# RWKV chunks of a hybrid decoder layer: sixteen at once with crosswise odd ones, and the state carried by transition matrices

## The reference

```python
    def step(s, inp):
        r_t, w_t, k_t, v_t, a_t, b_t = inp
        sa = jnp.einsum('nhvk,nhk->nhv', s, a_t)
        s = (s * w_t[:, :, None, :] + sa[..., None] * b_t[:, :, None, :]
             + v_t[..., None] * k_t[:, :, None, :])
        return s, jnp.einsum('nhvk,nhk->nhv', s, r_t)
```

## Time and profile before

| | us |
|---|---|
| median of 3 runs | 2684.76 |
| lowest, highest | 2681.96, 2686.89 |
| the profiled execution | 2676.91 |
| its span | 2675.2 |

### The profile page before, as it was taken

One profiled execution on the slowest core, in us unless ns is written; L12 is line 12 of the kernel. 1 busy time (PEld: TensorE's weight loads), 2 busy tenths in 40 slices (PEclk: granted clock), 3 DMA queues, 4 the chain that ended last, 5 costly groups with the idle time before them and its releaser, 6 DMA issues.

```text
span 2675.2 us, 39291 instructions
## 1 busy us (share of the span) xinstructions
PE 2428.9 (91%) x17425; PEld 1629.9 (61%) x17425; DVE 925.3 (35%) x1626; ACT 457.0 (17%) x946; POOL 158.9 (6%) x269
## 2 busy tenths in 40 slices
PE   5998999898888898888879997999999999999994
PEld 3665665557656766756756664666666666666563
DVE  3962441035325415415514333333331013333222
ACT  4114121122113113113130001111110001111002
POOL 2700000000000000000100000000000000000001
PEclk8999999999998998998979998999999999999997
DMA  6101233410020020011033311111101011110101
GB/s 220 60 20 41 78 120 111 132 56 16 11 58 15 8 61 15 8 38 46 3 137 106 128 32 32 32 33 33 33 29 44 24 64 33 33 33 25 36 20 65
DMA packets 111367, 139.72 MB, mean 52 GB/s; under 512 B 14818, under 2 KB 85975, under 8 KB 111184
## 3 DMA queue, kind: packets, MB, share of 16 engines
q1 hardware_dynamic: 96512, 115.38, 13.3%
q10 hardware_dynamic: 10992, 15.21, 1.6%
q0 software_dynamic: 3696, 6.64, 0.9%
HBM read 117.59 MB, written 19.61 MB: 51 GB/s over the span
## 4 chain that ended last, share of the span: by engine, by line
PE 79%; DVE 11%; ACT 4%; DMA 3%; issue 2%; DVEq 0%; ACTq 0%; SPq 0%; POOL 0%; POOLq 0%
PE ps L623 77%; DVE arena L1669 5%; DVE arena L1672 2%; DMA W<-in_w_in_dram 2%; PE ps L627 1%; DMA arena<-in_x_prompt_dram 1%; ACT Y L1437 1%; DVE arena L2100 1%; ACT arena L1316 0%; DMA Y<-in_x_prompt_dram 0%; DVE hT L1672 0%; DVE hT L1669 0%; DVE arena L2037 0%; ACT arena L1362 0%; DVE s5v L1669 0%
## 5 line engine op out<-in xcount | busy, mean ns | idle before, releaser
L623 PE MATMUL ps<-hT,W 128*128 128x352 f32 x4368 | 1337.1, 467 | 53.7 <-DMA W<-in_w_in_dram 17.8
L623 PEld LDWEIGHTS ps<-hT,W 128*128 128x128 f32 x4368 | 837.0, 193 | 528.8 <-issue 58.3
L623 PE MATMUL ps<-arena,W 128*128 128x352 f32 x1440 | 432.0, 463 | 14.7 <-DVE arena L1669 11.9
L623 PE MATMUL ps<-arena 64*64 64x64 f32 (+6 forms) x8744 | 354.6, 232 | 55.2 <-DVE arena L1669 22.0
L623 PEld LDWEIGHTS ps<-arena,W 128*128 128x128 f32 x1440 | 276.1, 192 | 170.1 <-DVE arena L1669 12.5
L623 PEld LDWEIGHTS ps<-arena 64*64 64x64 f32 (+3 forms) x8744 | 300.7, 137 | 115.7 <-issue 43.0
L1316 ACT ACTIVATE arena<-ps 128x512 f32<-128x512 f32 (+7 forms) x235 | 113.2, 489 | 523.1 <-PE ps L623 318.9
L2214 DVE TENSOR_SCALAR Y<-Y,PAR 128x1024 f32<-128x1024 f32 x88 | 49.0, 557 | 426.4 <-ACT Y L1316 424.7
L1316 ACT ACTIVATE Y<-ps 128x352 f32<-128x352 f32 (+3 forms) x220 | 69.9, 350 | 715.2 <-PE ps L623 536.5
L1669 DVE TENSOR_TENSOR arena<-arena 128x1056 f32<-128x1056 f32 (+6 forms) x181 | 166.8, 922 | 59.8 <-PE ps L623 44.9
L1669 DVE TENSOR_TENSOR arena<-ps,arena 128x256 f32<-128x256 f32 (+3 forms) x188 | 99.0, 527 | 220.4 <-PE ps L623 164.0
(11 more groups left out here) (250 smaller groups left out, 995.7 us busy)
## 6 DMA issues: line engine op xcount, KB each, us to landing
W<-in_w_ada_dram SPq DMA_DIRECT2D x12, 2048.0 KB, 9.4
W<-in_w_up_dram SPq DMA_DIRECT2D x22, 1024.0 KB, 6.5
gates<-arena ACTq DMA_DIRECT2D x72, 176.0 KB, 1.8
arena<-gates SPq DMA_DIRECT2D x24, 528.0 KB, 3.5
W<-in_w_in_dram SPq DMA_DIRECT2D x17, 512.0 KB, 4.9
W<-in_w_in_dram SPq DMA_DIRECT2D x4, 1536.0 KB, 7.1
W<-in_w_down_dram SPq DMA_DIRECT2D x4, 1536.0 KB, 6.6
W<-in_w_in_dram SPq DMA_DIRECT2D x5, 1024.0 KB, 6.5
```

The source lines that it names most:

```text
L623: return nc.tensor.matmul(out, lhsT, rhs, start=start, stop=stop, skip_group_check=True)
```

## The change

All 16 chunks of a pass are handled together, and odd chunks cross: where an operand lies on the partitions of head h, the product of an odd chunk is written to the other half (side), or the other way round, while two chunks next to each other write different banks. Exceptions are the transposed products of the levels (zt) and the turn of A, which stay in their own half, and the chain. A level works in two halves of eight chunks, with X and XT updated as 512 columns at a time. X is preset by ACT with the identity, and DVE writes the first factors over it with a predicated copy; XT is made by turning X on PE instead of from LA.

After level 5 four sets of products over all 16 chunks make, besides the old quantities, Gm (a transition matrix for each chunk, with the identity added) and R + YT.LA in ARp, and put the state-free part of outputs and of state updates into PSUM. The chain is then one accumulating product of Gm with the last state, and one DVE operation that scales it by PC into Sb, for 15 steps; the second product of a step adds the state's part to the output. Vt, Bt, Kt and the others get new places in the arena (VB, W0, U0, YT, Gm, Sb), partly over Bp, Kp, Vp and Z, and decode gets its own small tiles (dX, dXT, dLT, dYb, dLTm).

In decode gate group 5 goes to bank 7, group 6 is cut after three k steps instead of four and its first part moved ahead of the wait for dec_made 2, group 7 runs whole before the wait for dec_made 4, group 8 is cut in two, ahead of the output head sums and behind the turn of the decode states. The last prompt state is turned at the end of the pass. ACT has one more instruction a pass, the fill of X.

PE's core of the change:

```diff
-                for bt in range(2):
-                    for x, (b, src) in enumerate(((0, Vp), (1, Bp), (2, Kp))):
-                        take(b)
-                        for c in range(8):
-                            m = heads(lambda hp: mm(pb[b][hp, 64 * c:64 * c + 64], src[hp, 8 * bt + c, :], idS[hp, :]))
...
+                def both(bt):
+                    for c in range(8 * bt, 8 * bt + 8):
+                        for hh in range(2):
+                            yield c, c % 2, c % 8 // 2, half_of(hh), side(c, hh)
+
+                take(0, 1)
                 for bt in range(2):
+                    for c, par_, i, hp, sd in both(bt):
+                        m = mm(pb[par_][sd, col64(c // 2)], ARp[hp, c, 0, :], Bp[hp, c, :])
+                m.then_inc(sem("la_done"), 1)
+                give("la_ev", 0, 1)
+
+                def with_a_r(src, bt):
+                    b = 4 + 2 * bt
+                    take(b, b + 1)
+                    for c, par_, i, hp, sd in both(bt):
+                        m = mm(pb[b + par_][sd, P * i:P * (i + 1)], src[hp, c, :],
+                               ARp[hp, c, :, :].rearrange("p a b -> p (a b)"))
...
+                with_a_r(Bp, 0)
+                with_a_r(Bp, 1)
+                take(2, 3)
...
+                values_b(0)
+                with_a_r(Kp, 0)
+                with_a_r(Kp, 1)
+                values_b(1)
+                pe.wait_ge(sem("la_ev"), 5 * j + 1)
+                for bt in range(2):
+                    take(2 * bt, 2 * bt + 1)
+                    for c, par_, i, hp, sd in both(bt):
+                        m = mm(pb[2 * bt + par_][hp, col64(i)], X[sd, pos(c), :], idS[sd, :])
+                    m.then_inc(sem("tk_done"), 1)
+                    give("tk_ev", 2 * bt, 2 * bt + 1)
+                take(4, 5)
+                for bt in range(2):
+                    for c, par_, i, hp, sd in both(bt):
+                        m = mm(pb[4 + bt][hp, col64(4 * par_ + i)], ARp[hp, c, 0, :], idS[hp, :])
+                m.then_inc(sem("tk_done"), 1)
...
+                def yy(l, s):
+                    pe.wait_ge(sem("lt_ready"), level_at(j, l, s))
+                    if l > 1:
+                        pe.wait_ge(sem("zx_ev"), 8 * j + 2 * (l - 2) + s + 1)
+                    take(2 * s, 2 * s + 1)
+                    for c, par_, i, hp, sd in both(s):
+                        m = mm(pb[2 * s + par_][hp, col64(i)], LT[sd, lane(c), :], X[sd, pos(c), :])
...
+                def zt(l, s):
+                    zt_ready(l, s)
+                    take(4 + s)
+                    for c, par_, i, hp, sd in both(s):
+                        m = mm(pb[4 + s][hp, col64(4 * par_ + i)], Yb[hp, lane(c), :], XT[hp, lane(c), :])
...
+                yy(1, 0)
+                yy(1, 1)
+                for l in range(1, last):
+                    for s in range(2):
+                        zx(l, s)
+                        zt(l, s)
+                        yy(l + 1, s)
...
+                take(6, 7)
+                for s in range(2):
+                    for c, par_, i, hp, sd in both(s):
+                        m = mm(pb[6 + par_][hp, col64(c // 2)], YT[sd, pos(c), :], vb(c, 1)[sd, :])
+                m.then_inc(sem("gm_done"), 1)
+                give("gm_ev", 6, 7)
...
+                for c in range(1, 16):
+                    par_, i = c % 2, c // 2
+                    pe.wait_ge(sem("s_ready"), 16 * j + c)
+                    if c == 1:
+                        pe.wait_ge(sem("gm_ev"), 2 * j + 1)
+                    heads(lambda hp: mm(pb[4 + par_][hp, col64(i)], Gm[hp, pos(c), :], Sb[hp, c - 1, :], False, True))\
+                        .then_inc(sem("ds_done"), 1)
+                    if c == 1:
+                        pe.wait_ge(sem("y_part"), j + 1)
+                        pe.wait_ge(sem("gm_ev"), 2 * j + 2)
+                    m = heads(lambda hp: mm(pb[par_][hp, col64(i)], Sb[hp, c - 1, :], ARp[hp, c, 1, :], False, True))
+                m.then_inc(sem("ry_done"), 1)
```

DVE's and ACT's part of it, the mask on POOL and the decode order:

```diff
@@ POOL
-                        if n > 2:
-                            pool.wait_ge(sem("yy_done"), 2 * (n - 2))
-                        pool.tensor_tensor(LT[n % 2], LA[:, :, 0, :],
+                for l in range(1, LEVELS):
+                    for s in range(2):
+                        if l == 1:
+                            pool.wait_ge(sem("la_ev"), 5 * j + s + 2)
+                        else:
+                            pool.wait_ge(sem("yy_done"), level_at(j, l - 1, s))
+                        pool.tensor_tensor(LT[:, 8 * s:8 * s + 8, :], LA[:, 8 * s:8 * s + 8, 0, :],
@@ ACT
+                copy(X[:, :, :], idS[:, :].unsqueeze(1).to_broadcast([P, 16, RCH])).then_inc(sem("x_unit"), 1)
...
+                act.wait_ge(sem("tk_done"), 6 * (j + 1))
+                copy(LTm[:].rearrange("p c t -> p (c t)"), ps[:, 4:6, :].rearrange("p b t -> p (b t)"))\
+                    .then_inc(sem("tk_ev"), 1)
@@ DVE
+                step(v.copy_predicated(X[:, :, :], m_l0[:].bitcast(words).unsqueeze(1).to_broadcast([P, 16, RCH]),
+                                       ps[:, 0:2, :].rearrange("p b (c t) -> p (b c) t", t=RCH)), "la_ev")
...
+                def carry(c):
+                    step(v.tensor_scalar(Sb[:, c, :], pb[4 + c % 2][:, col64(c // 2)], PC[:, c:c + 1], None, MUL), "s_ready")
...
+                for c in range(1, 16):
+                    dve.wait_ge(sem("ds_done"), 15 * j + c)
+                    carry(c)
@@ PE, decode
-                gates_part(8 + j, 5, 0, KT, 2)
+                gates_part(8 + j, 5, 0, KT)
...
+                gates_part(8 + j, 6, 0, 3)
                 pe.wait_ge(sem("dec_made"), 4 * j + 2)
...
-                gates_part(8 + j, 6, 0, KT // 2)
+                gates_part(8 + j, 6, 3, KT)
...
-                gates_part(8 + j, 6, KT // 2, KT)
+                gates_part(8 + j, 7, 0, KT)
...
-                gates_part(8 + j, 7, 0, KT, 3)
+                gates_part(8 + j, 8, 0, 4)
...
-                gates_part(8 + j, 8, 0, KT, 4)
+                gates_part(8 + j, 8, 4, KT)
```

More of the change, by code:

```diff
@@ new lines, in _ @@
+                pe.wait_ge(sem("la_ev"), 5 * (j + 1))
+                pe.wait_ge(sem("tk_ev"), 6 * j + 3)
+                take(6, 7)
+                for s in range(2):
+                    for c, par_, i, hp, sd in both(s):
+                        m = mm(pb[6 + par_][hp, col64(c // 2)], KA[sd, lane(c), 0, :], vb(c, 0)[sd, :])
+                m.then_inc(sem("wy_done"), 1)
+                give("wy_ev", 6, 7)
+                for s in range(2):
+                    zt(last, s)
+                pe.wait_ge(sem("tk_ev"), 6 * (j + 1))
@@ new lines, in _ @@
+                for s in range(2):
+                    pe.wait_ge(sem("zt_ev"), level_at(j, last, s))
+                    if s == 0:
+                        take(0, 1)
+                    for c, par_, i, hp, sd in both(s):
+                        m = mm(pb[par_][sd, col64(c // 2)], XT[hp, lane(c), :], LTm[hp, lane(c), :])
+                    if s:
+                        m.then_inc(sem("wy_done"), 1)
+                        give("wy_ev", 0, 1)
+                    else:
+                        take(2, 3)
+                        pe.wait_ge(sem("wy_ev"), 2 * j + 1)
+                    for c, par_, i, hp, sd in both(s):
+                        m = mm(pb[2 + par_][sd, col64(c // 2)], XT[hp, lane(c), :], W0[hp, pos(c), :])
@@ new lines, in _ @@
+                m.then_inc(sem("gm_done"), 1)
+                give("gm_ev", 6, 7)
+                pe.wait_ge(sem("u0_ev"), j + 1)
+                for s in range(2):
+                    for c, par_, i, hp, sd in both(s):
+                        m = mm(pb[4 + par_][hp, col64(c // 2)], vb(c, 1)[sd, :], U0[sd, pos(c), :], False, False)
+                m.then_inc(sem("gm_done"), 1)
+                readers["s_ready"] = 16 * j + 15
+                give("s_ready", 4, 5)
+                take(2, 3)
@@ L1551, in _ @@
[L1551 to L1559 removed]
+                    act.wait_ge(sem("tk_done"), 6 * j + 2 + bt)
@@ L2107, in _ @@
+                y = Y[:, 2 + j, :]
+                for par_ in range(2):
+                    step(v.tensor_copy(y[:, 0:TP].rearrange("p (c a t) -> p a c t", a=2, t=RCH)[:, par_],
+                                       pb[par_].rearrange("p (c t) -> p c t", t=RCH)), "ry_ev" if par_ else "dve_step")
                 dve.wait_ge(sem("dec_done"), 7 * j + 2)
```

385 lines of the change are left out of this document (167 added, 218 removed).

## The result

The changed kernel takes 2643.74 us (median of 4, 2641.86 to 2648.57), the kernel before on the same chip 2683.38: a ratio of 0.9853, with a 95% interval of 0.9836 to 0.987. That is 40 us faster. The forecast was 119 us faster, 2566, with 2596 as the upper end. The direction is right, two thirds of the gain are missing.

What follows compares the result with a forecast made beforehand. PE was taken to bound the kernel in four RWKV stretches, 328.7 us together. New stretches of 51.1 + 2.8 us save 113.1, decode 5.6, 118.7 in all: 2676.9 becomes 2558.2, as a median 2566 us, range 2546 to 2596.

Steps and rivals of the forecast that it cites:

- steps 1 to 3: RWKV stretch ahead of the chain: front 11.8 us, levels 20.9, tail products 7.5, with crosswise records at 14.6 ns.
- rival C: RWKV stretches: crosswise order gives no gain in long runs; a stretch of 74.1 us, median 2658; chance 0.08.
- The working that gave 81.1 for 81.2: Same queue-by-queue working applied to a stretch of the kernel before: 81.1 us where the trace has 81.2.
- The wide records: Front, moving operands of 128 columns: 28 ns crosswise, bounds 28 and 56; the other end adds 3.6 us a stretch.
- The rule weighed: Skill's rule that different row tiles cannot use one PSUM bank at once; by it crosswise order would gain nothing.
- The side queues: ACT and POOL in a stretch: POOL's masks hidden with 1.6 us to spare, ACT waits of 0.9 and 1.1 us.
- Rival E: Stretches: POOL and ACT masks or copies end 3 to 6 us later; 2578 to 2590; chance 0.14 together with another rival.
- Step 4: Chain: 15 steps with one round trip each, 0.76 us a step, 10.9 us a stretch.
- Step 5: Clock falls inside the new chain and comes back in the dense decode work, costing 2.8 us a stretch.
- Rival A: Chain: the clock stays full, its gaps being 0.5 us; 4 x 2.8 less, 2555 us; chance 0.14.
- Step 6: Decode: the same gate groups, otherwise cut, cover PE's waits; 1.4 us a pass saved.
- Step 7: ACT's fill of X (about 1.03 us), ahead of the decay sigmoids, costs nothing; uncovered 1 us a pass.

Runs made afterwards that it cites:

- e4: Changed kernel with two more pairs of products that nobody reads in each of 14 chain steps: 2627.8 us.
- g1: Changed kernel with gate group 5 moved from decode into the chain, in halves of 176 columns: 2624.2 us, timed again 2624.9.
- e8: Changed kernel with gate groups 5 and 6 moved from decode into the levels, 2 or 3 products after each of seven level steps: 2648.3 us.
- e7: Changed kernel with gate groups 5 and 6 moved from decode into the chain as whole products: 2637.4 us.
- m0: Changed kernel with tail products that share their stationary operand merged into crosswise products of 128 columns: 2628.5 us, ratio to before 0.9795.
- e5: Changed kernel with 256 more crosswise records a pass in the levels, from products that nobody reads: 2678.8 us.

## Why the prediction was wrong

Against its own steps, second pass (by the order of the records, the first product stands at 831.5, the first level product at 844.6, the first tail product at 876.1, the first chain product at 889.6 and the first decode product at 902.5):

| step | forecast | trace after |
|---|---|---|
| 1 front | 11.8 | 13.1 |
| 2 levels | 20.9 | 31.5 |
| 3 tail products | 7.5 | 13.5 |
| 4 and 5 chain, its clock | 10.9 + 0.9 | 12.9 |
| sum | 52.0 | 71.0 |

**The step that failed** is the rate under steps 1 to 3. I took 14.6 ns a crosswise record from a burst of 64 and used it for two thousand in a row. The rate is right for 127 records; beyond that the supply gives 29 to 32 ns. Steps 1 to 3 alone are 17.9 us short, most of it in the levels and the tail; with the chain's part it is 19.6 a stretch in the mean of four, 78 us in all, nearly the whole error of the forecast. "the new kernel runs some 400 in a row" stood in the text as the argument for rival C, with a chance of 0.08. C's time, 2658, is the nearest to what came, for a reason that C does not name: crossing is not without gain, it pays 6.3 us a stretch. The trace of before could not show the floor. Its 480 records in 15.82 us are 33 ns each and not 29, but the difference is waits, as I had taken it: at four places, one a level and so 96 records apart and not 128, there are 0.35 us from one start to the next. The working that gave 81.1 for 81.2 proved nothing of the supply either, because on the diagonal array and supply go at almost one pace. At 30 to 33 ns a record for all 2000 ahead of the chain, a stretch would have come to 72 to 78.

**The wide records** crosswise, for which I took 28 ns between bounds of 28 and 56, took 28 in a burst.

**The rule weighed.** Rows after show crosswise products of both heads into different partitions of one bank at 15 ns, in each burst of 127. The Trainium skill, "TensorEngine Tiling (Array Packing)", section Restrictions and Gotchas, excludes this for row tiles on one bank; here too the trace disagrees, and the loss has another cause, the supply.

**The side queues were right:** in the second pass ACT holds PE up for 1.6 us in two waits, where 2.0 were listed, and POOL's masks for 0.5 in three. Rival E did not come. The longer wait for ACT (1.4 us, to 842.27) also stands at the end of a block and ends 1.6 us after a packet, so it can be the supply's.

**Step 4:** a step is 0.79 us at full clock against 0.76; the PE part of it starts later than I read from the old chain. A small miss, 0.4 us a stretch.

**Step 5 was right in kind and too small.** The clock falls inside the chain and returns in decode; it costs 4.6 us a pass (e4), not 2.8, because it stays down up to 17 us. Rival A is refuted. Records per us, by which I had reasoned, are not the mark: g1's chain has 10 in 0.87 us, hardly more than the 8 in 0.76 of my sum, and keeps its clock in three passes, with PE never idle. The Trainium skill, "TensorE: Matmul & The Clock Gate", section Why this matters for your kernels, warns of idle gaps between bursts. That idle time counts agrees with e4, where the fall goes when products fill the gaps, and with g1's last pass, where it follows a stop of 1.93 us. But I had drawn rival A from that warning, and gaps of only 0.34 us, one a step, were enough here; and the 30 us at half with no gap, in g1, it does not explain.

**Step 6 was right.** At full clock (e4) decode with its sums is 22.5 + 5.4 = 27.9 us, against 101.8 - 81.2 + 8.8 = 29.4 before: 1.5 less, forecast 1.4. In the changed kernel itself the slow clock takes more than that back.

**Step 7** has no trace of a cost: from the last head sums of a pass to the first of the next, where ACT's fill lies, PE needs 65.3 us in the second pass before and 65.3 after.

## What to carry to other kernels

A rate read from a burst holds for a burst. When a change makes short instructions shorter, look in a long run of them for the pace at which instructions arrive, and count instructions before columns: merging products that share their stationary operand paid the whole 30 ns of each record saved, crossing quarters a quarter of what the burst rate promised. Engine time without instructions (one long product) is partly free where PE waits for instructions: in e8's levels 4.7 of 11.6 us were. In a chain of round trips it also holds the clock; it should be no longer than the idle part of a step, for in e7, where it was longer, the step grew from 0.79 to 1.17 us.

## What I had not expected of the hardware

In long runs of short products PE stops after each 127 or 128 records, which are 256 instructions, and goes on 3.4 to 4.1 us after the last start, each time 1.2 to 1.6 us after a packet of 16.4 KB has landed on the instruction queue q8. That queue has one packet for each 256 of PE's instructions (144 for 36923, 140 for m0's 35907, 152 for e5's 38975), and a packet takes 1.1 us. The next one starts only some 1.3 us after PE has gone on; why not sooner, and how many blocks are held in stock beyond the one that a lump of 128 records showed, stays open. A full-width f32 record of 128 columns takes 118 ns where a crosswise one of as many columns takes 28, and a change from full-width products to quarters and back costs about 0.27 us. The clock can stay at half for some 30 us while PE has no idle time at all.
